# Two matmul tiles behind each of two norms on the undivided activation, all squares added on VectorE, and a weight chunk's high part copied earlier

## What is computed

```python
h = rmsnorm(x, g_attn[l]) * (1.0 + sc1) + sh1          # first norm
proj = h @ w_in[l]                                      # ... attention, mixed
x = x + ga1 * (mixed @ w_out[l])
h2 = rmsnorm(x, g_ffn[l]) * (1.0 + sc2) + sh2           # norm behind w_out
gate, up = jnp.split(h2 @ w_gu[l], 2, axis=-1)
x = x + ga2 * ((jax.nn.silu(gate) * up) @ w_down[l])
x = rmsnorm(x, g_final)                                 # norm behind w_down
h = rmsnorm_2(x, norm_g[l]) * (1.0 + scale) + shift     # and the next one on it
u = h @ w_in_2[l]                                       # cv, cg, cs, lx, ls
v = causal_depthwise_conv(cv * jax.nn.sigmoid(cg), dw_w[l], dw_b[l])   # 31 taps
v = jax.nn.silu(layernorm(v, cln_g[l], cln_b[l])) @ pw2_w[l] + pw2_b[l]
x = x + (1.0 + gate) * (jnp.concatenate([v * silu(cs), y_lru], -1) @ w_out[l])
return rmsnorm_2(x, final_g)
```

## Time and profile before

| | us |
|---|---|
| median of three runs | 1058.04 (1057.92 to 1058.24) |
| the profiled execution | 1059.21 |
| its span, first to last instruction | 1057.4 |
| PE busy | 1037.7 |
| DVE busy | 628.8 |
| POOL busy | 472.2 |
| ACT busy | 421.4 |

### The profile page before, as it was taken

One profiled execution on the slowest core, in us unless ns is written; L12 is line 12 of the kernel. 1 busy time (PEld: TensorE's weight loads), 2 busy tenths in 40 slices (PEclk: granted clock), 3 DMA queues, 4 the chain that ended last, 5 costly groups with the idle time before them and its releaser, 6 DMA issues.

```text
span 1057.4 us, 14026 instructions
## 1 busy us (share of the span) xinstructions
PE 1037.7 (98%) x5222; PEld 838.3 (79%) x5222; DVE 628.8 (59%) x1223; ACT 421.4 (40%) x585; POOL 472.2 (45%) x176
## 2 busy tenths in 40 slices
PE   7999999999999999999999999999999999999997
PEld 5787796767878888888888888888887777888886
DVE  5367997786562432223337101679999999864322
ACT  4244325884241222212232222423435888362232
POOL 0034342692324443443533443347674766633340
PEclk9999999999999999999999999999999999999999
DMA  9984231140424335434374223223322222323212
GB/s 327 349 273 137 80 116 45 42 161 1 146 92 147 133 119 171 147 131 147 119 228 150 90 100 109 81 79 122 117 80 80 80 80 87 114 80 101 98 40 80
DMA packets 127250, 128.91 MB, mean 122 GB/s; under 512 B 3552, under 2 KB 125280, under 8 KB 127200
## 3 DMA queue, kind: packets, MB, share of 16 engines
q1 hardware_dynamic: 125952, 127.38, 36.9%
q10 hardware_dynamic: 1248, 0.86, 0.3%
HBM read 126.13 MB, written 2.10 MB: 121 GB/s over the span
## 4 chain that ended last, share of the span: by engine, by line
PE 53%; issue 33%; POOL 10%; DMA 1%; ACT 1%; SPq 1%; DVE 0%; POOLq 0%; DVEq 0%; ACTq 0%
PE bank L715 11%; PE bank L717 11%; PE bank L716 11%; POOL w_lo L589 10%; PE bank L1061 2%; PE bank L1032 2%; PE bank L904 2%; PE bank L1256 1%; PE bank L1257 1%; PE bank L1255 1%; DMA ada_stage<-in_w_ada 1%; PE bank L1213 1%; PE bank L922 1%; PE bank L740 1%; PE bank L741 1%
## 5 line engine op out<-in xcount | busy, mean ns | idle before, releaser
L589 POOL TENSOR_TENSOR w_lo<-w_stage,w_hi 128x2048 fp32r<-128x2048 f32 x77 | 368.8, 4790 | 489.2 <-ACT w_hi L1326 489.2
L715 PE MATMUL bank<-act_hi,w_hi 128*128 128x512 f32 x848 | 335.2, 395 | 0.5 <-POOL w_lo L589 0.4
L717 PE MATMUL bank<-act_hi,w_lo 128*128 128x512 f32 x848 | 330.1, 389 | 0.0
L716 PE MATMUL bank<-act_lo,w_hi 128*128 128x512 f32 x848 | 330.0, 389 | 0.0
L1326 ACT ACTIVATE w_hi<-w_stage 128x2048 fp32r<-128x2048 f32 x78 | 149.3, 1914 | 250.0 <-PE bank L717 236.2
L715 PEld LDWEIGHTS bank<-act_hi,w_hi 128*128 128x128 f32 x848 | 159.3, 188 | 39.2 <-issue 5.8
L717 PEld LDWEIGHTS bank<-act_hi,w_lo 128*128 128x128 f32 x848 | 159.1, 188 | 33.5
L716 PEld LDWEIGHTS bank<-act_lo,w_hi 128*128 128x128 f32 x848 | 159.3, 188 | 33.2 <-issue 1.4
L2167 DVE SCALAR_TENSOR_TENSOR bank<-v_pad,vcol,bank 128x512 f32<-128x512 f32 x208 | 138.2, 746 | 0.0
L2079 DVE TENSOR_TENSOR tmp<-bank,tmp 128x512 f32<-128x512 f32 x22 | 15.2, 692 | 157.0 <-PE bank L717 153.6
L715 PE MATMUL bank<-ff_hi,w_hi 128*128 128x512 f32 x176 | 69.7, 396 | 0.0
(11 more groups left out here) (317 smaller groups left out, 1533.7 us busy)
## 6 DMA issues: line engine op xcount, KB each, us to landing
w_stage<-in_w_in SPq DMA_DIRECT2D x29, 1024.0 KB, 5.1
w_stage<-in_w_gu SPq DMA_DIRECT2D x22, 1024.0 KB, 5.1
ada_stage<-in_w_ada SPq DMA_DIRECT2D x20, 1024.0 KB, 11.6
w_stage<-in_w_out SPq DMA_DIRECT2D x12, 1024.0 KB, 5.1
ada_stage<-in_mod_w SPq DMA_DIRECT2D x12, 1024.0 KB, 7.6
w_stage<-in_w_down SPq DMA_DIRECT2D x8, 1024.0 KB, 5.2
late_stage<-in_w_ada SPq DMA_DIRECT2D x4, 1024.0 KB, 9.2
w_stage<-in_pw_w SPq DMA_DIRECT2D x4, 1024.0 KB, 5.1
```

What stands on the lines that cost most here:

```text
L589: nc.gpsimd.tensor_tensor(w_lo[b][:], w_stage[b][:], w_hi[b][:].bitcast(F32), ALU.subtract).then_inc(s_lo, 1)
L715: pe.matmul(dst, wh, rhs_hi(k), start=(first and k == 0), stop=False)
L716: pe.matmul(dst, wh, rhs_lo(k), start=False, stop=False)
L717: mm = pe.matmul(dst, wl, rhs_hi(k), start=False, stop=(last and k == n_k - 1))
```

## The change

- **Tiles on undivided x.** The two tiles of the first chunk behind the norms of w_out and of w_down no longer wait for the norm. ACT makes raw_hi = xT times scale for each slice, DVE the remainder raw_lo, behind each residual; PE multiplies them (`undivided`): slices 0 to 2 before the sums, 3 and 4 between sums and spread, 5 to 7 behind the spread. Behind `normed`, DVE copies the spread deviation to SBUF (rstd) and multiplies the two banks by it into tmp[0] and tmp[1]; ACT's Silu or Sigmoid takes them with a bias. For w_out's norm, raw parts have buffers of their own; for w_down's, they lie in act_hi and act_lo, and ACT overwrites a slice once PE is done with it (s_rawused).
- **The shift as a bias.** DVE multiplies the first chunk's w_stage by the shift, eight steps of 256 columns (`gate_bias_rows`, `bias_rows`), and PE turns the row with two products of one column. SP's refill of that w_stage buffer behind w_out's norm waits for it (s_bias). The loop of w_gu's DMAs has its first pass written out for that.
- **Squares.** In the first three of the four norms, DVE also adds the square of slice 7, and PE sums once.
- **Products of ones** (keep_warm) are gone from the two norms.
- **The third chunk's w_hi** is copied by ACT ahead of the high parts of slices 6 and 7, not after them and the first activations.
- **Order behind w_out.** ADA_TILE is 9, so four rows are summed in the first four tiles; the modulations needed for the scale are ready from tile 5. Tiles 4 to 7 use the banks in another order.

Core of the diff (left out: semaphores, buffers, and the unchanged shape of the rest):

```diff
-ADA_TILE = 6
+ADA_TILE = ADA_ITEMS
+NORMS = 4
...
             sp.wait_ge(s_res, 1)
-            with sp.Fori(2, KF // 2 + 2) as j:
+            w_dma(C_GU, w_cols(a["w_gu"], 0, KD, 0))
+            w_dma(C_GU + 1, w_cols(a["w_gu"], 0, KD, D_FF))
...
+            sp.wait_ge(s_bias, 1)
+            with sp.Fori(3, KF // 2 + 2) as j:
...
-                plain = 0 if gained else 6
-                if gained:
-                    pe.wait_ge(s_gsqused, KD - 2)
-                    sums(7, tmp[2], True, False)
-                pe.wait_ge(s_sqused, (KD - 2) * j)
-                sums(plain, rstd, True, False)
+                plain, last = 2 if gained else 6, j == NORMS
+                if last:
+                    pe.wait_ge(s_sqused, (KD - 1) * j - 1)
+                    sums(plain, rstd, True, False)
                 if before:
                     before()
                 if gained:
-                    pe.wait_ge(s_gsq, KD)
-                    sums(7, tmp[3], False, True).then_inc(s_gcol, 1)
-                pe.wait_ge(s_sq, KD * j)
-                sums(plain, tmp[1], False, True).then_inc(s_col, 1)
+                    pe.wait_ge(s_gsqused, KD - 1)
+                    sums(7, tmp[2], True, True).then_inc(s_gcol, 1)
+                    pe.wait_ge(s_res, 2 * KD - 1)
+                pe.wait_ge(*((s_sq, KD * j) if last else (s_sqused, (KD - 1) * j)))
+                sums(plain, tmp[1] if last else rstd, not last, True).then_inc(s_col, 1)
...
-            square_sums()
-
+                if t == 5:
+                    pe.wait_ge(s_bias, 1)
+                    pe.wait_ge(s_mod, 5)
+                    for c in range(2):
+                        mm = pe.matmul(bank[7][:, NCOL + c:NCOL + c + 1], ada2_acc[:, c * P:(c + 1) * P], ones[:, 0:1],
+                                       start=True, stop=True)
+                    mm.then_inc(s_rowmm, 1)
...
+            square_sums(before=first_gates, meanwhile=lambda: gates((3, 4)))
+            gates(range(5, KD))
             pe.wait_ge(s_res, KD)
...
-            b0, b1 = C_GU % 2, (C_GU + 1) % 2
-            low, high = slice(0, P), slice(P, 2 * P)
-            pe.wait_ge(s_lo, C_GU + 1)
-            two, third = [(bank[0][:], b0, low, s_guacc), (bank[1][:], b0, high, s_wused)], [(bank[2][:], b1, low, s_guacc)]
-            abreast(two, 1, range(KD // 2))
+            b1 = (C_GU + 1) % 2
             pe.wait_ge(s_lo, C_GU + 2)
-            abreast(third, 1, range(KD // 4))
-            abreast(two, 1, range(KD // 2, KD))
-            abreast(third, 1, range(KD // 4, KD))
-            tile(bank[3][:], b1, high, KD, hi, lo).then_inc(s_wused, 1)
+            abreast([(bank[2][:], b1, low, s_guacc), (bank[3][:], b1, high, s_wused)], 1)
             gu_modulations(0)
...
                 for k in range(KD):
+                    if k == KD - 2:
+                        hi_part(early, early % 2, early // 2)
+                    if held and k < KD - 1:
+                        act.wait_ge(s_rawused, k + 1)
...
+                if k == KD - 4:
+                    gate_bias_rows()
...
+                for c in {KD - 2: range(3), KD - 1: range(3, KD - 1), KD: (KD - 1,)}.get(k, ()):
+                    dve.wait_ge(s_mod, 5)
+                    dve.wait_ge(s_rawhi, c + 1)
+                    V.scalar_tensor_tensor(raw_lo[:, c, :], xT[:, c, :], scale1[:, 1, c:c + 1], raw_hi[:, c, :].bitcast(F32),
+                                           ALU.mult, ALU.subtract).then_inc(s_rawlo, 1)
...
             normed(1, SH2, bank[4], (5, 7))
+            link(V.tensor_copy(rstd[:], bank[4][:]))
+            for m in range(2):
+                dve.wait_ge((s_guacc, s_wused)[m], (1, C_GU + 1)[m])
+                V.tensor_tensor(tmp[m][:], bank[m][:], rstd[:], ALU.mult).then_inc(s_div, 1)
 
             ada_steps = steps[0]
...
             normed(0, SH3, bank[6], (5, 7))
+            link(V.tensor_copy(rstd[:], bank[6][:]))
+            for m in range(2):
+                dve.wait_ge((s_i2acc, s_wused)[m], (1, C_IN2 + 1)[m])
+                V.tensor_tensor(tmp[m][:], bank[m][:], rstd[:], ALU.mult).then_inc(s_div, 1)
             dve.wait_ge(s_spread, 4)
```

More of the change, by code:

```diff
@@ L1183, in _, with first_undivided @@
                             late_products(b)
-            square_sums(gained=True)
+                        if (m2, g, m) == (KD // 2 - 1, 2, 0):
+                            pe.wait_ge(s_adaacc, len(ADA_ORD) + 1)
+                            for c in range(2):
+                                mm = pe.matmul(bank[7][:, NCOL + c:NCOL + c + 1], ada2_acc[:, c * P:(c + 1) * P], ones[:, 0:1],
+                                               start=True, stop=True)
+                            mm.then_inc(s_adamm, 1)
+            b0, b1 = C_IN2 % 2, (C_IN2 + 1) % 2
+            seconds = lambda ks: undivided(1, b0, (act_hi, act_lo), s_i2acc, ks)
+            def first_undivided():
+                pe.wait_ge(s_lo, C_IN2 + 1)
+                pe.wait_ge(s_res, 2 * KD - 2)
+                seconds((0, 1, 2))
+            square_sums(gained=True, before=first_undivided, meanwhile=lambda: seconds((3, 4)))
+            seconds(range(5, KD))
             pe.wait_ge(s_res, 2 * KD)
[L1187 to L1190, removed]
             pe.wait_ge(s_lo, C_IN2 + 2)
[L1192 to L1195, removed]
+            abreast([(bank[2][:], b1, low, s_i2acc), (bank[3][:], b1, high, s_wused)], 2)
             with pe.Fori(1, KD // 2) as j:
@@ L1750, in ada_step @@
                     else:
-                        dve.wait_ge(s_late_ada[late], 16)
+                        dve.wait_ge(s_ada[late], 16 * (ADA_BUF.count(late) + 1))
                     dve.wait_ge(s_adaacc, o)
@@ L2027, in _, with bias_rows @@
             added = [0]
+            def bias_rows():
+                dve.wait_ge(s_stage[C_IN2 % 2], C_IN2 // 2 * 16 + 16)
+                for t in range(KD):
+                    src, w, part = w_stage[C_IN2 % 2][:, t, :], modc(SH3 + t), bank[7][:, 0:NCOL]
+                    if t == 0:
+                        V.tensor_scalar(part, src, w, None, ALU.mult).then_inc(s_adastep, 1)
+                    else:
+                        dve.wait_ge(s_adastep, steps[0] + t)
+                        V.scalar_tensor_tensor(ada2_acc[:] if t == KD - 1 else part, src, w, part, ALU.mult, ALU.add).then_inc(
+                            s_adaacc if t == KD - 1 else s_adastep, 1)
             def residual(n0, gain, groups=1, gained=False, banks=range(4), between=0, chunks=()):
@@ L2045, in residual_2, with gate_bias_rows @@
                                        ALU.mult, ALU.add).then_inc(s_res, 1)
-            ada_done[0] = 0
-            residual(C_OUT, lambda k: modc(GA1 + k), banks=OUT_BANK, between=ADA_TILE, chunks=list(range(ADA_ATT, ADA_OUT)))
-            dve.wait_ge(s_adamm, ADA_DVE)
-            ms = slice(2 * ADA_ATT, 2 * ADA_OUT)
-            V.tensor_tensor(mod[:, ms], bank[7][:, ms], vcol[:, ms], ALU.add).then_inc(s_mod, 1)
-            dve.wait_ge(s_mod, 4)
-            fold("g_ffn", SC2, 1)
+            def gate_bias_rows():
+                dve.wait_ge(s_adaacc, ADA_DVE)
+                dve.wait_ge(s_stage[C_GU % 2], C_GU // 2 * 16 + 16)
+                for t in range(KD):
+                    src, w, part = w_stage[C_GU % 2][:, t, :], modc(SH2 + t), bank[6][:, 0:NCOL]
+                    if t == 0:
+                        V.tensor_scalar(part, src, w, None, ALU.mult).then_inc(s_adastep, 1)
+                    else:
+                        dve.wait_ge(s_adastep, steps[0] + t)
+                        V.scalar_tensor_tensor(ada2_acc[:] if t == KD - 1 else part, src, w, part, ALU.mult, ALU.add).then_inc(
+                            s_bias if t == KD - 1 else s_adastep, 1)
+                steps[0] += KD - 1
```

128 lines of the change are left out of this document (104 added, 24 removed).

## The result

The changed kernel takes 1062.79 us (median of 5 runs, 1062.77 to 1064.03) against 1057.92 for the kernel before on the same chip (5 runs): a ratio of 1.005, 95% interval 1.0038 to 1.0061. It is 4.9 us slower, where 6.65 us of gain were predicted. Its profiled execution has a span of 1061.0, only 3.6 above that of before. The rest of the 4.9 is luck of one execution: the profiled execution of before took 1059.21, 1.2 above its median.

The account below looks back on a forecast made before the run. PE, busy 98% of the span, was taken to bound the kernel, with 14.9 us at two norms open to attack. Gains of 1.5 + 4.3 + 0.85 = 6.65 us from 1058.04 gave 1051.4, range 1049.6 to 1056.2.

Parts of the forecast that it names:

- Norm behind w_out, PE's order: Behind w_out: four tiles end 5.3 us earlier, but a new wait at the modulations takes 3.8, leaving 1.5 us gained.
- The remainders' meeting with the w_lo: Behind w_out: DVE's first three remainders wait for POOL's w_lo until 287.6; slice 7's square, added about 296.6, just fits.
- rival 2: The clock falls in the new wait at the modulations, costing about 1.7 us: 4.9 us gained, 1053.1; chance 0.18.
- Norm behind w_down, PE: Behind w_down: PE's four tiles end at 692.84 where the next started at 697.62, a lead of 4.8 us.
- Norm behind w_down, DVE: DVE's chain decides; its short convolution loses 3.3 us to POOL rather than 6.6, putting DVE 3.7 us ahead.
- shrinks: A smaller meeting of DVE and POOL behind the short convolution, at 790, shrinks too; no size given.
- The term of 4.3 us: Gain of the norm behind w_down: DVE's 3.7 us plus the fourth gate's slack of 0.7, rounded down.
- Rival 4: Slower: remainders and shifted convolution meet whole w_los, at 774 to 860 or 284 to 288, 4.35 us each; chance 0.05.
- two give 1063: Within rival 4: from 1055.0, one meeting of 4.35 us loses the gain and two give 1063.
- rival 1: DVE keeps the lead small: 3.0 gained, 1055.0; chance 0.18; sign: PE waits over 1 us in total between 780 and 900.
- Third norm: The third norm loses one sum, 0.89 us, taken as a gain of 0.85.
- The sum: Whole kernel: 1.5 + 4.3 + 0.85 = 6.65 us gained, giving 1051.4; chance 0.53.

Follow-up runs that it names:

- the run with idle products: Changed kernel with 14 idle products of 128x128, two records each, ahead of the first MLP modulations, where PE waits: 1061.14 us.
- the best kernel: Changed kernel, modulations two tiles later, w_lo's of C_IN2 + 7, +10, +11 in quarters, +13 held until the second short convolution is done: 1051.21 us.
- quarters alone: Changed kernel with POOL making the w_lo's of ten w_in_2 chunks (C_IN2 + 4 to C_IN2 + 13) in four instructions each: 1059.32 us.
- three delays: Changed kernel, modulations two tiles later, with 0, 10 or 21 idle products behind the fourth tile of w_in_2: 1057.75, 1060.23 and 1052.29 us.
- the run with four quarters: Changed kernel, modulations two tiles later, w_lo's of C_IN2 + 7, +10, +11 and +12 in quarters, +13 whole: 1053.97 us.

## Why the prediction was wrong, point by point

- **Norm behind w_out, PE's order: right.** The new wait at the modulations was put at 3.6 us and is 3.16; the tile behind it was to be 1.5 earlier and is 1.4 (2.5 less the 1.1 of luck). The remainders' meeting with the w_lo was there: POOL is at it from 282.49 to 287.1, and the first three remainders take 5.33 us for the 2.2 of three free ones. It used up the slack: the last square is added by 295.78 and the sum starts at 295.83, about 0.25 us later than forecast once the 1.1 of luck are put back.
- **The clock there: wrong, a term that the sum put at nothing; it was rival 2.** Its price was put at 1.7, and it cost 1.75 in the trace and 1.65 in the run with idle products. I had given it 0.18. With it the norm behind w_out gives nothing that is left (1.4 - 1.75), and the whole forecast would have been 1053.1.
- **Norm behind w_down, PE: right.** Lead of 4.8 predicted, 4.7 measured; the early w_hi did its part, as no wait for w_lo is left at the fifth tile.
- **Norm behind w_down, DVE: the step that failed.** I worked out where DVE and POOL would stand at one place, the short convolution, and took DVE to arrive there at 774.0. It arrived at 775.59; counted from the first tap, which came 1.0 earlier than I had it, that is 2.6 us late, because I had missed the meeting at 740.56, where the convolution's instruction reads `conv` from SBUF beside a tap. I had taken it that POOL's w_lo of 772.7 would end at 777.3 and cost 3.3; it came at 774.32, after tap sums that were themselves late (they need DVE's v_pad), and the one behind it, which I hadn't placed at all, ran through the short convolution from 781.90. 7.3 us were lost there instead of 3.3 (12.3 for 5.04), and 3 more at 792.52, where I had written that the meeting "shrinks". The term of 4.3 us was worth about minus 5.2: after was 0.75 ahead at the end of w_down and 4.47 behind at the mean sums.
- **Rival 4, slower, 0.05: this happened,** beside rival 2. Its mechanism and its place (774 to 860) were right; it was one place wider, from 740 on. That its "two give 1063" is the measured time is luck: it counts two meetings of 4.35 us from 1055.0, where the runs have 2.9, 3.0 and 0.8 us more in meetings and 1.75 of clock, which it leaves out. The argument against it, PE's short waits in the trace of before, said nothing: in the phase of before the pair at 742.16 just missed its w_lo. The sign named for rival 1 showed too: PE's waits between 780 and 900 add up to 7.9 us, 6.7 of them at the third gate. Having written that DVE's chain decides, I should have walked all of POOL's w_lo's through DVE's chain with the new times; the rows for it were in the trace of before.
- **Third norm: right,** 0.89 for 0.85.
- **The sum:** the three terms as measured are minus 0.35 (1.4 - 1.75), minus 5.2 and 0.89, together minus 4.7 against the 4.9 by which the kernel got slower. With both losses mended, each at a price, it took 1052.29 (4.85 us of idle products) and 1051.21 (one w_lo 2.04 us late). That this is near the forecast 1051.4 is luck and bears out no term: later modulations gave 5.0 us that the forecast doesn't have. Of the 6.84 us by which the best kernel beats the one before, 4.7 (5.04 - 0.35) are the norm behind w_out and 0.9 the third, which leaves some 1.3 for the norm behind w_down, not 4.3.

Open is how much of the 1.3 us by which quarters alone missed their interval was the clock and how much the second short convolution, and what a w_lo in quarters that is also held back would give; neither was tried. Nor did any run touch the meeting at 852 us in before: its pair takes 6.0 us where a free one takes 1.4, in the best kernel too (844.09).

## What to carry to other kernels

When two engines hold each other up, as DVE and POOL do here, and one of them follows a third, write out both timelines with the new times over the whole stretch that the lead reaches, and look at every pair; a lead of PE is a shift of phase for everybody who serves it, and the best of three delays here was the longest. Where a change gives PE a new wait, count a fallen clock behind it as part of the wait's price: here it came behind waits of 3.16, 2.16 and 2.04 us, and not behind those of 2.44 and 2.19. And if a kernel gets faster by giving PE idle work, or slower by being ahead, try to hold back the engine that disturbs rather than PE: 1051.21 against 1052.29 us here.

## What the runs showed of the hardware

- A DVE instruction with two SBUF inputs that is issued while POOL works on a w_lo (two SBUF inputs too) waits until POOL's instruction ends, and the w_lo itself gets little longer (4.6 to 4.9, at most 5.5): 5.75 us for two instructions that take 1.41 free, ending 0.55 behind the w_lo. Where POOL's tap sums, which have two SBUF inputs as well, follow the w_lo at once, the second of the two is held again: the pair of 740.56 ends 2.3 us behind the w_lo, and that of 736.92 as long behind its own. Taps that take their sum from PSUM run beside the same w_lo at their usual 0.66 us. A `TENSOR_SCALAR` on l_pad is held too (5.29 us for two that take 0.99), though it reads a single tensor; writing SBUF it takes 0.5 us, where the first taps, which write PSUM, take 0.76 (697.23 of after: 1.52 for two). The Trainium skill, "GPSIMD Engine Reference", section Specifications, names contention for two SBUF inputs and for a two-port perf mode; the faster `TENSOR_SCALAR` may be the second case, which no run here separates. The size, the whole of the other engine's instruction, is from the runs.
- It goes the other way as well: in the run with 21 idle products and the modulations later, DVE was first, and POOL stood behind six DVE instructions, at no cost to the end:

```profile
806.11 1.00 DVE L2335 TENSOR_SCALAR tmp<-l_pad,vcol 128x512 f32<-128x512 f32 x2
807.02 4.05 DVE L2338 SCALAR_TENSOR_TENSOR tmp<-l_pad,vcol,tmp 128x512 f32<-128x512 f32 x6
...
807.14 9.60 POOL L607 TENSOR_TENSOR w_lo<-w_stage,w_hi 128x2048 fp32r<-128x2048 f32 x1 [10.25 <-ACT w_hi L1381]
```

- A wait of PE of 3.16 us brought the clock down to its lower level (1.2 GHz of 2.4) for what cost 1.65 to 1.75 us; the length of the wait alone doesn't say it: waits of 2.44 and 2.19 us at the gates left 810 to 830 us at 1.00 in the run with four quarters, while one of 2.16 us in the run with all quarters (0.66 in 820 to 825) and one of 2.04 us in the run with the held w_lo (0.66 in 815 to 820) brought it down.
